# The three output projections by Strassen's scheme on pairs of token tiles, with the residual rows in a ring of four tiles

## The reference

```python
    o = o * jax.nn.silu(z.astype(jnp.float32))
    return o.astype(h.dtype) @ w_out          # mixer output, (1024 x 1024) @ (1024 x 1024)
...
            y = _fox_mixer(h, k, v, F, b_w_in[j], q_norm_g[j], b_w_out[j])
            x = x + gate * y                  # gate: one row of 1024 from c
...
h = _rms(x, g) * (1.0 + scale) + shift        # input of the next layer, of the new x
```

## Time and profile before

| | |
|---|---|
| time, median of 3 runs (lowest, highest) | 4646.5 us (4646.17, 4651.3) |
| span of the profiled execution | 4654.6 us |
| TensorE busy | 4342.8 us, 93% |
| VectorE busy | 1647.6 us, 35% |
| ScalarE busy | 1008.1 us, 22% |
| granted TensorE clock, mean over the span | 0.966 |
| bout, start to last product | 120.4 us |
| eout | 151.7 us |
| oout | 120.7 us |

### The profile page before, as it was taken

How to read it: one execution, slowest core, us unless ns; L and a number is a source line. 1 busy time by engine, 2 the same in 40 slices (tenths; PEclk the granted TensorE clock), 3 DMA queues, 4 the chain that set the end, 5 groups by cost and what they waited for, 6 DMA issues and landing times. The chain is left out here.

```text
span 4654.6 us, 63706 instructions
## 1 busy us (share of the span) xinstructions
PE 4342.8 (93%) x25960; PEld 3110.1 (67%) x25960; DVE 1647.6 (35%) x4208; ACT 1008.1 (22%) x2270; POOL 230.5 (5%) x281
## 2 busy tenths in 40 slices
PE   7996899999999999996999999989999995999996
PEld 3443546888665587643888888868656644888885
DVE  5408224433784355724111111133345524111111
ACT  2011122212664224622000000031135521000001
POOL 0100000000220000000000010000000000000000
PEclk9997999999999999997999999999999997999998
DMA  7658211222431122015677777731251013888887
GB/s 277 235 92 324 98 46 38 85 98 100 154 110 46 43 83 89 29 64 208 249 256 257 255 255 264 256 130 41 84 192 37 1 56 118 317 309 321 319 309 259
DMA packets 132952, 756.89 MB, mean 163 GB/s; under 512 B 13728, under 2 KB 52384, under 8 KB 97296
## 3 DMA queue, kind: packets, MB, share of 16 engines
q1 hardware_dynamic: 107248, 669.78, 39.6%
q0 software_dynamic: 20272, 64.76, 4.8%
q10 hardware_dynamic: 5232, 19.63, 1.2%
HBM read 663.46 MB, written 91.19 MB: 162 GB/s over the span
## 5 line engine op out<-in xcount | busy, mean ns | idle before, releaser
L2845 PEld LDWEIGHTS psum<-arena,w_ring 128*128 128x128 f32 x8192 | 1020.9, 192 | 15.0 <-issue 15.0
L2845 PE MATMUL psum<-arena,w_ring 128*128 128x160 f32 (+1 forms) x8192 | 1025.3, 288 | 4.2 <-ACT arena L2927 2.7
L401 PE MATMUL psum<-w_ring,arena 128*128 128x512 f32 (+3 forms) x1576 | 619.1, 550 | 11.7 <-PEq L196 8.3
L401 PEld LDWEIGHTS psum<-w_ring,arena 128*128 128x128 f32 x1576 | 297.5, 192 | 301.2 <-issue 272.5
L2860 PE MATMUL psum<-w_ring,arena 128*128 128x512 f32 x1024 | 450.0, 592 | 0.0
L429 PE MATMUL psum<-w_ring,arena 128*128 128x256 f32 (+1 forms) x2016 | 435.3, 376 | 13.5 <-PEq L196 7.1
L429 PEld LDWEIGHTS psum<-w_ring,arena 128*128 128x128 f32 x2016 | 377.7, 192 | 64.7 <-issue 15.6
L2986 DVE TENSOR_TENSOR arena<-arena,psum 128x320 f32<-128x320 f32 (+1 forms) x128 | 58.2, 455 | 963.8 <-PE psum L2845 963.8
L401 PE MATMUL psum<-arena,w_ring 128*128 128x512 f32 (+1 forms) x880 | 376.0, 583 | 2.8 <-DVE arena L334 1.7
L2911 ACT ACTIVATE arena<-psum 128x320 f32<-128x320 f32 (+1 forms) x128 | 52.6, 411 | 1309.1 <-PE psum L2845 1309.1
L2860 PEld LDWEIGHTS psum<-w_ring,arena 128*128 128x128 f32 x1024 | 189.7, 190 | 215.0 <-issue 215.0
(11 more groups left out here) (380 smaller groups left out, 3441.4 us busy)
## 6 DMA issues: line engine op xcount, KB each, us to landing
w_ring<-in_wstream SPq DMA_DIRECT2D x258, 2048.0 KB, 7.8
x_rows<-arena SPq DMA_DIRECT2D x26, 512.0 KB, 2.7
w_ring<-in_wstream ACTq DMA_DIRECT2D x6, 2048.0 KB, 7.7
xn_rows<-arena POOLq DMA_DIRECT2D x18, 512.0 KB, 2.9
arena<-f_rows SPq DMA_DIRECT2D x8, 1024.0 KB, 7.6
arena<-x_rows SPq DMA_DIRECT2D x2, 4096.0 KB, 21.4
arena<-x_rows SPq DMA_DIRECT2D x8, 1024.0 KB, 9.3
arena<-in_x_first SPq DMA_DIRECT2D x4, 1024.0 KB, 21.8
```

The lines of the kernel that those rows point to most:

```text
L401: last = cr.nc.tensor.matmul(bank_ap, l, r, start=(k == 0), stop=(k == len(pairs) - 1))
L2845: last = nc.tensor.matmul(half(bank0 + v)[:, c], w[:, k, m * P:(m + 1) * P], xT[:, k, :], start=(k == 0), stop=(k == KT - 1))
```

## The change

`block_out` computes the eight latent tiles by `Quads`: four pairs of tiles (q, q+4), two column halves, so N = 8 quads and nine turns of the loop. The context tiles of eout keep the old products and now come first. New on VectorE are the sums of weight halves (`sums_56`, `sums_74`, four operations 1024 wide for each half), the sums of a pair's mixer rows (`row_sums`, four operations 512 wide for each pair), and `add_rows`, which multiplies and adds a finished quad (2 x 512) in SBUF. A quad's results pass through `stage`, a buffer of two, so `act_1` of quad n waits for `add_rows` of quad n-2. `Follow` now handles tiles in pairs. The x rows lie in a ring of four tiles: two pairs are loaded before the stage, and the other two from DRAM when the first two are stored.

The core of the diff. What is not shown: the two weight-sum functions and the gates at the head of each engine's list, which keep their work.

```diff
+        self.deviation(act, n)
+        self.scaled(act, n)
+    def deviation(self, act, n):
+        act.wait_ge(self.var, n + 1)
+        self.cr.nc.scalar.activation(self.stat[:, 2, n:n + 1], self.stat[:, 1, n:n + 1], ACT.Sqrt).then_inc(self.std, 1)
...
+PAIRED = [i for q in range(4) for i in (q + 4, q)]
+def x_slot(i):
+    return 2 * (i % 2) + i // 4
+def first_x(cr, rows):
+    return [(x_ring(cr)[:, x_slot(i)], rows[i * P:(i + 1) * P, :]) for i in (4, 0, 5, 1)]
...
     def ready(eng, i):
-        if i < nt:
-            eng.wait_ge(fol.fin, i + 1)
+        if i < NT:
+            q = i % 4
+            eng.wait_ge(added, 2 * q + 2 if q < 3 else 8 + (i < 4))
+        elif nt > NT:
+            eng.wait_ge(fol.fin, i - NT + 1)
         else:
             eng.wait_ge(x_in, 16)
...
+        w = cr.w(w0 + t)
+        left = {1: mixer_half(0, q), 2: mixer_half(1, q), 4: mixer_half(1, q + 4), 5: S[q][0], 6: S[q][1], 3: S[q][2], 7: mixer_half(0, q + 4)}
+        right = {1: w[:, 0:4, 0:256], 2: w[:, 4:8, 0:256], 3: w[:, 4:8, 256:512], 7: w[:, 0:4, 256:512],
+                 5: T[t][0], 6: T[t][1], 4: T[t][2]}
+        return lambda p: [(left[p][:, k], right[p][:, k]) for k in range(4)]
...
+            for q in range(4):
+                for i in (q + 4, q):
+                    ready(sp, i)
+                    sp.dma_start(x_d[i * P:(i + 1) * P, :], row_of(i)).then_inc(x_st, 16)
+                if q < 2:
+                    sp.wait_ge(fol.xnr, pair_of(q)[1] + 1)
+                    sp.wait_ge(x_st, 16 * 2 * (q + 1))
+                    for i in (q + 6, q + 2):
+                        sp.dma_start(row_of(i), x_from[i * P:(i + 1) * P, :]).then_inc(x_ld, 16)
...
+            for t in range(2):
+                cr.wait_w(pe, w0 + t)
+            for n, i in enumerate(ctx_tiles):
                 for t in range(2):
-                    if i == 0:
-                        cr.wait_w(pe, w0 + t)
                     w = cr.w(w0 + t)
                     product(cr, pe, un, un.bank(un.n), [(of_mixer(k, i), w[:, k, :]) for k in range(KT)])
-                    if i == 0 and t < len(gates):
-                        pe.wait_ge(d_ok, t + 1)
-                        if t:
-                            pe.wait_ge(g_ok, 2 * t)
-                        gate_rows(cr, diag[:, t], (6, 7), g_mm)
-                    for n in of_half(2 * i + t):
-                        fol.pe(pe, n)
-                for g in range(len(groups)):
-                    if groups[g][1] == i - 1:
-                        if g == 0:
-                            pe.wait_ge(g_ok, 2 * len(gates))
-                        logits(g)
+                    if n == 0:
+                        gates_of(t)
+            if NC:
+                pe.wait_ge(un.empty, NC)
+            for n in range(N + 1):
+                if n < N:
+                    qd.pe_open(pe, n, factors(n))
+                    if n == 0 and not NC:
+                        gates_of(0)
+                if n == 1 and lead:
+                    fol.pe(pe, 0)
+                if n >= 4 and n % 2 == 0:
+                    fol.pe(pe, pair_of(n // 2 - 2)[0])
+                if n:
+                    if n <= 2:
+                        pe.wait_ge(w_sum, 2 * n)
+                    qd.pe_third(pe, n - 1, factors(n - 1))
+                if n == 1 and lead:
+                    fol.pe(pe, 1)
+                if n >= 4 and n % 2 == 0:
+                    fol.pe(pe, pair_of(n // 2 - 2)[1])
+                if n < N:
+                    if n <= 1:
+                        pe.wait_ge(w_sum, 2 * n + 1)
+                    if n % 2 == 0:
+                        pe.wait_ge(x_sum, n // 2 + 1)
+                    qd.pe_second(pe, n, factors(n))
+                if n == 3 and first_group == 1:
+                    logits(0)
+                if n == 7 and groups:
+                    logits(first_group)
+                if n:
+                    qd.pe_close(pe, n - 1, factors(n - 1))
...
+            fol.pe(pe, pair_of(3)[0])
+            fol.pe(pe, pair_of(3)[1])
...
             for n in range(lead):
                 fol.squares(act, n)
                 fol.normed(act, n)
...
+            for n in range(N + 1):
+                if n < N:
+                    if n >= 2:
+                        act.wait_ge(added, n - 1)
+                    qd.act_1(act, n, blocks(n)[0])
+                if n == 0 and not NC:
+                    copy_gate(0)
+                if n == 1 and lead:
+                    fol.act_tile(act, 0)
+                if n >= 3 and n % 2:
+                    for m in pair_of((n - 3) // 2):
+                        fol.squares(act, m)
+                if n >= 4 and n % 2 == 0:
+                    fol.act_tile(act, pair_of(n // 2 - 2)[0])
+                if n:
+                    qd.act_3(act, n - 1, blocks(n - 1)[3])
+                if n >= 3 and n % 2:
+                    for m in pair_of((n - 3) // 2):
+                        fol.deviation(act, m)
+                if n == 1 and lead:
+                    fol.act_tile(act, 1)
+                if n >= 4 and n % 2 == 0:
+                    fol.act_tile(act, pair_of(n // 2 - 2)[1])
+                if n < N:
+                    qd.act_2(act, n, blocks(n)[1])
+                if n == 4 and first_group == 1:
+                    copy_logits(0)
+                if n == 8 and groups:
+                    copy_logits(first_group)
+                if n:
+                    qd.act_21(act, n - 1, blocks(n - 1)[2])
+                if n >= 3 and n % 2:
+                    for m in pair_of((n - 3) // 2):
+                        fol.scaled(act, m)
+            for m in pair_of(3):
+                fol.squares(act, m)
+                fol.normed(act, m)
+            for m in pair_of(3):
+                fol.act_tile(act, m)
+            if groups:
+                copy_logits(first_group + 1)
...
+            def row_sums(q):
+                if q >= 2:
+                    dve.wait_ge(qd.fifth, 2 * (q - 1))
+                x11, x12, x21, x22 = mixer_half(0, q), mixer_half(1, q), mixer_half(0, q + 4), mixer_half(1, q + 4)
+                ln(tt(S[q][0], x21, x22, ALU.add))
+                ln(tt(S[q][1], S[q][0], x11, ALU.subtract))
+                tt(x21, x11, x21, ALU.subtract)
+                tt(S[q][2], x12, S[q][1], ALU.subtract).then_inc(x_sum, 1)
+            def add_rows(n, r=None):
+                q, t = n // 2, n % 2
+                if r is None:
+                    dve.wait_ge(qd.made11, n + 1)
+                    dve.wait_ge(qd.made12, n + 1)
+                if r == 0:
+                    dve.wait_ge(qd.made12, n + 1)
+                if r != 0:
+                    dve.wait_ge(qd.made22, n + 1)
+                    dve.wait_ge(qd.made21, n + 1)
+                if q >= 2:
+                    dve.wait_ge(x_ld, 32 * (q - 1))
+                some = slice(0, 2) if r is None else slice(r, r + 1)
+                k = some.stop - some.start
+                y, x = stage[:, n % 2, some], xr[:, 2 * (q % 2):2 * (q % 2) + 2, t * 512:(t + 1) * 512][:, some]
+                ln(tt(y, y, gate[:, 0, t * 512:(t + 1) * 512].unsqueeze(1).broadcast_to([P, k, 512]), ALU.mult))
+                tt(x, x, y, ALU.add).then_inc(added, 1)
...
+            else:
+                sums_56(0)
+                row_sums(0)
+                gate_diag(cr, diag[:, 0], *gates[0], d_ok)
+                for m in range(lead):
+                    fol.dve_var(dve, m)
+                    fol.dve_rst(dve, m)
+            if NC:
+                dve.wait_ge(g_ok, 2 * len(gates))
+                for n, i in enumerate(ctx_tiles):
+                    for t in range(2):
+                        residual_add(cr, dve, ln, un, 2 * n + t, tmp, gate[:, 1, t * 512:(t + 1) * 512],
+                                     Xc[:, i, t * 512:(t + 1) * 512], fol.fin if t else None)
+                    if n == 0:
+                        row_sums(0)
+                    fol.dve_var(dve, n)
+                    fol.dve_rst(dve, n)
+            for n in range(N + 1):
+                if n < N:
+                    if n == 1:
+                        sums_56(1)
+                    qd.dve_11(dve, n, blocks(n)[0])
+                    if n <= 1:
+                        if n and not NC:
+                            dve.wait_ge(g_mm, 1)
+                        sums_74(n)
+                if n == 1 and lead:
+                    fol.dve_tile(dve, 0)
+                if n >= 4 and n % 2 == 0:
+                    fol.dve_tile(dve, pair_of(n // 2 - 2)[0])
+                if n:
+                    qd.dve_22(dve, n - 1, blocks(n - 1)[3])
+                if n >= 3 and n % 2:
+                    for m in pair_of((n - 3) // 2):
+                        fol.dve_var(dve, m)
+                    for m in pair_of((n - 3) // 2):
+                        fol.dve_rst(dve, m)
+                if n == 1 and lead:
+                    fol.dve_tile(dve, 1)
+                if n >= 4 and n % 2 == 0:
```

(55 more changed lines are left out.)

136 lines of the change are left out of this document (79 added, 57 removed).

## The result

| | before | changed |
|---|---|---|
| time, median (lowest to highest), 10 runs each | 4645.7 us (4641.9 to 4653.9) | 4660.8 us (4653.9 to 4666.3) |
| ratio | | 1.0028, 95% interval 1.0020 to 1.0036 |
| span of the profiled execution | 4654.6 us | 4658.6 us |
| TensorE / VectorE / ScalarE busy | 4342.8 / 1647.6 / 1008.1 us | 4306.6 / 1726.0 / 1040.6 us |

The change makes the kernel slower by 15 us by the medians, and by 13 us (9 to 17) by the ratio. The forecast was 4661.5 us, with slower at 0.62. TensorE has 36 us less to do and the kernel takes longer, so the page of the profile alone shows that the saving was lost in waits. The two spans differ by 4.0 us only, since the profiled execution of the kernel before lies 8 us above its median.

A forecast was written before the change was run, and what follows sets the result against it. TensorE, busy 93% of the span, was taken to set the time. Saving -39.8, turns +20.2, starts +20.2 and ends +6.9 gave +7.5 us; the clock's 7.5 made +15, 4661.5 us, range 4638 to 4679.

The forecast's parts named there:

- The saving: Three output stages: eight latent tiles take 96.6 us of TensorE instead of 109.9; 13.3 us saved each, 39.8 in all.
- The waits in the turns: Turns 2, 4, 6 and 8: TensorE waits for VectorE 1.25, 1.7, 1.7 and 2.1 us; 20.2 us in all.
- The starts: Stage starts and turn 1: TensorE waits add oout 1.4, bout 14.5, eout 4.35 us, together 20.2.
- The 1.4 us before the gates' product: Start of bout and oout: VectorE's sums and diagonals take 6.9 us where p1 and p2 end at 5.5.
- the 9 us wait: bout, turn 0: p5 waits 9.3 us for dve_11 behind the context tiles, then TensorE restarts at the lower clock, 1.9 more.
- the prediction's list of signs: Profile after: expected gaps in named places, and stretches from start to last product near 129, 151 and 116 us.
- The ends: After the last product: 2.4 us more in oout, 3.1 in eout, 1.4 in bout; together 6.9 us.
- The clock: Waits of turns 1, 4, 6 and 8: four of eleven drop TensorE's clock, costing 7.5 us.
- Rival 1: Output stages: the same waits, but the clock holds; +7.5 us, time 4654; chance 0.22.
- Rival 2: Turns 1, 4, 6 and 8: every one of the eleven waits drops the clock; +28 us, time 4675; chance 0.13.
- Rival 3: dve_12 to dve_11: the turns' waits don't come about, VectorE free by E + 4.5; -16.5 us, 4630; chance 0.16.
- Rival 4: Ring of x rows: reload of the next pair is late, 5 us for each of two reloads per stage; +30; chance 0.04.

The follow-up runs named there:

- e7_waits_filled: Changed kernel with the edits of e1_ctx_later and e2_row_sums_early, gate diagonals first, logits products moved from turn 7 to 8; 4626.1 us, 0.9949 of before.
- e1_ctx_later: Changed kernel with bout's context-tile squares and scalings moved behind the first quad's copies, VectorE's part likewise; 4649.9 us, 1.0002 of the kernel before.
- e2_row_sums_early: Changed kernel with row_sums moved ahead of dve_12 and the residual addition in odd turns; 4645.0 us, 0.9994 of the kernel before.

## Why the prediction was right

**The saving.** 12.08 us for a quad, whatever the stage, was the term, and it holds. In e7_waits_filled, whose middle turns wait for nothing, two turns with two groups of transposes last 25.93 us (the 32 records at 1498.67 to those at 1524.60):

```profile
1498.67 7.07 PE L437 MATMUL psum<-w_ring,arena 128*128 128x256 f32 x32
...
1524.60 7.07 PE L437 MATMUL psum<-w_ring,arena 128*128 128x256 f32 x32
```

2 x 12.08 + 2 x 0.87 is 25.90. With most waits filled the scheme is worth 23 us of its 39.8.

**The waits in the turns.** Shown are 1.09 for turn 2, 1.46 for 4 and 6, 1.92 for 8 and 1.63 for 1, where 1.25, 1.7, 2.1 and 1.9 were predicted. The time lost is longer than the idle time shown, since the last record's modelled end lies some 0.17 us behind the point where the next could start: the products at 1554.13 would have let the transposes start at 1555.86, 1.73 us later, and they start at 1557.94, 2.08 late. In the same way turn 2 lost 1.26, turns 4 and 6 1.65 (two such turns last 27.58 us, 1511.86 to 1539.44, and 25.93 without the wait), turn 1 1.79 and bout's start 9.3, which was 9.3 in the forecast too. In a stage 6.6 us against 6.75. VectorE's list was timed right as well: `dve_12` to `dve_11` takes 5.57 us in turn 2 (1472.90 to 1478.47), in the forecast 5.52.

**The starts.** The 1.4 us before the gates' product was mis-sized. The stage in the earlier trace rows begins at the lower clock, and p1 and p2 were put at 5.5 us. Here both bout and oout began at the full clock (16 records in 3.69), so TensorE came sooner to a wait whose end VectorE sets: 2.9. Where a stage did begin at the lower clock, in e1_ctx_later's bout (16 records in 5.08), the wait was 1.50. In bout the 9 us wait takes up whatever happens before it; the records behind it cost 2.4 us at the lower clock (16 in 6.11 in place of 3.69) where 1.9 were predicted, and the stretch came out at 129.1 against 129. In oout the clock fell behind the first wait (3.0 us), and once more in turn 8 (1.7), which makes the 120.3 of the stretch out of the predicted 116. eout has 150.4. The 151 of the prediction's list of signs doesn't follow from its own terms, 151.7 - 13.3 + 4.35 + 6.75 = 149.5. eout's two waits at the start are 0.85 and 0.80 as shown, about 1.0 and 1.1 lost, where 1.2 and 1.25 were predicted; its first 16 records took 7.10 in place of the 8.80 that it had before, and turn 8 lost 1.7 by the clock.

**The ends.** Last copy of the logits on ScalarE and the first matmul of the next block, oout of the changed kernel:

```profile
3872.08 0.60 ACT L2126 ACTIVATE arena<-psum 128x512 f32<-128x512 f32 x1 [3.95 <-PE psum L2049]
```
```profile
3874.02 1.06 PE L2863 MATMUL psum<-consts,arena 128*128 128x128 f32 x8 [2.00 <-PEq L196]
```

From the last product to that copy's end 15.3 us, predicted 15.8. But the next block begins 1.3 us after the copy, where it was 3.3 before, so the end of oout costs nothing instead of 2.4; eout's costs 2.0 instead of 3.1. The trace shows one more thing that the barrier waited for: the block also waits for the store of its last normed rows (`keep`), and in the kernel before that DMA was issued at 3858.02 and landed 8.8 us later, at 3866.8, 1.2 behind the copy. In the changed kernel it was issued at 3864.31 and landed 7.4 us later, 1.0 before the copy's end. So the forecast measured the end by the copy where this store was later. No run tries whether the store set the end. bout's end grew by 1.6 (predicted 1.4).

**The clock.** Four of the eleven short waits were to drop it, at 1.9 us each. Two did, in turn 8 of eout and of oout, at 1.7 each (from the transposes behind the wait to the second product behind it 4.31 us, and 2.63 in bout), and to these comes oout's start at 3.0, which wasn't counted. So 6.4 in place of 7.5, with nearly half of it in another place. That the two sums come so close is luck. None of the six waits of 1.46 did, nor the two of 1.63.

**Sum and rivals.** By stage +9, +1 and -3 were predicted, and the clock's 7.5 beside them; measured are +10.3, +0.7 and -0.3, +10.6 in the profiled pair. The medians are 15.1 us apart, while runs of one kernel lie 6 us to either side; bout alone cost 0.25% of 4649, 11.6 us, and the rest nothing, which is the stages' account. So the forecast's +15 agrees better with the median than with its own profiled pair. The 4 us that the stages don't account for lie within what one execution can't tell. By the stages the forecast was 4.4 us too high, 3.2 of it in the ends (3.7 in place of 6.9). The mechanism, waits on VectorE and on the context tiles in the places named, is shown; how near +15 came to the median is in part luck. Rival 1 (the clock holds) falls by the 8 records that took 3.44 us; it is nearer than the forecast by the profiled pair, where its +7.5 stands against +10.6. Rival 2 (all eleven drop) falls by the waits of 1.46 and 1.63. Rival 3 falls, since the waits came, but e2_row_sums_early shows the condition it named: with VectorE free in time, turns 2 to 7 run without a gap. Rival 4 falls, since no wait in the output stages ends on a DMA of x rows.

## What to carry to other kernels

Taking 40 us of work from the engine that sets the time lost 15 us, with every other engine below 40% busy: what decided was which independent work stood in front of the one operation it then waited for. So list for each turn what is queued ahead of the releasing instruction, move what has slack behind it, or give the waiting engine something in the gap that it has to do anyway. A wait taken away shows as a gain only if no later wait, ended by another engine or a DMA, takes it back.

## What the runs showed of the hardware

How a wait bears on the clock was counted over the changed kernel and the eight others in the output stages, one profiled execution each, for waits (idle time as shown) between stretches at the full clock. After waits of 0.8 to 1.65 us, in some 80 places, the records behind never took longer. The wait of turn 8, 1.92 us, stood in 19 places; in 8 of them the next records were slow, as 3.44 us for 8 above, in 11 they took 1.89. e1_ctx_later had it slow in three stages, e2_row_sums_early in none, with the same TensorE instructions around it. The two differ in the waits of turns 2, 4 and 6, which e2_row_sums_early doesn't have: in the kernels with them 7 of 12 places were slow, in those without 1 of 7. Whether these earlier waits matter is open; the count is too small to tell. A wait of 2.11 us in e7_waits_filled was followed by records at the full clock. Waits of 2.3 and 2.7 us were followed by slow records in 10 of 12 places, at 1.4 to 1.7 us each, and those of 2.8 to 2.9 us before the gates' product, shortly after the barrier, in 5 of 9. The granted clock behind a slow and a quiet one of the 1.92 us waits, first the changed kernel's turn 8 of oout, then e2_row_sums_early's of eout:

```profile
3852.50:3856.00 3.50, 3.50 (x11) 2.82 (x10) 0.84 (x3) 2.17 (x6) 0.00 (x0) 0.58 0.93 368
```
```profile
2117.00:2121.00 4.00, 3.21 (x15) 2.47 (x14) 2.51 (x7) 2.46 (x7) 0.00 (x0) 1.00 0.92 355
```

0.58 is mostly the lower of the two levels, 1.2 GHz; 1.00 is 2.4 GHz. So near 2 us the same gap costs nothing or 1.7 us from place to place, and waits below 1.7 us were always free of that price in these traces. The clock has a part in the spread between runs of one kernel: of 26 runs of the kernel before, the four with a mean granted clock of 0.964 averaged 4653.2 us and the six with 0.967 4646.0. How much of that these gaps make isn't shown. The Trainium skill ("TensorE: Matmul & The Clock Gate", HAM oscillation) shows the loss on a loop in which DMA waits recur between short bursts of matmuls. Here a single wait was enough, with 25 us of matmuls without any ahead of it (3824.67 to 3849.38 in the changed kernel).
